# Two chunked recurrences: small TensorE products ordered by tile shape, and in-chunk products made once per 128 tokens

## The reference

```
A = where(causal, q_in @ k_in^T, 0)            # inside one chunk
o = A @ v + q_in @ S_prev                      # in-chunk part + part from the state
S = dec * S_prev + k_out^T @ v                 # the state that goes on
```

```
sa = S_t-1 a_t
S_t = S_t-1 * w_t + sa b_t^T + v_t k_t^T
y_t = S_t r_t
```

## Time and profile before

| | |
|---|---|
| median of 3 runs | 3005.89 us (3000.68 to 3006.42) |
| the profiled execution | 2999.36 us |
| its span, first to last instruction | 2997.6 us |
| mean granted TensorE clock | 0.93 |
| stage of the recurrences, first step 1 to the last step 8 | 917.28 to about 981.9 us |

### The profile page before, as it was taken

One profiled execution on the slowest core, in us unless ns is written; L12 is line 12 of the kernel. 1 busy time (PEld: TensorE's weight loads), 2 busy tenths in 40 slices (PEclk: granted clock), 3 DMA queues, 4 the chain that ended last, 5 costly groups with the idle time before them and its releaser, 6 DMA issues. The chain is left out here.

```text
span 2997.6 us, 61808 instructions
## 1 busy us (share of the span) xinstructions
PE 2594.2 (87%) x22240; PEld 2419.3 (81%) x22240; DVE 1988.2 (66%) x4119; ACT 1347.4 (45%) x2439; POOL 643.0 (21%) x506
## 2 busy tenths in 40 slices
PE   5798677798399589999999999866899999999998
PEld 2598556468397588999988899865899999988997
DVE  5501632341652469599999966546596899999765
ACT  5632334234320265655544455523555555444554
POOL 0144124227200379100000000162593000000000
PEclk9899779799696799999999999987999999999999
DMA  9522012115100234544434355421344544443452
GB/s 302 179 91 79 1 39 75 59 57 156 42 1 1 72 132 163 180 157 155 161 141 146 140 180 184 136 89 36 128 168 168 169 154 154 145 148 141 171 193 98
DMA packets 153851, 374.20 MB, mean 125 GB/s; under 512 B 8656, under 2 KB 102880, under 8 KB 137088
## 3 DMA queue, kind: packets, MB, share of 16 engines
q1 hardware_dynamic: 150784, 367.59, 36.1%
q10 hardware_dynamic: 2944, 4.98, 0.5%
HBM read 371.49 MB, written 1.05 MB: 124 GB/s over the span
## 5 line engine op out<-in xcount | busy, mean ns | idle before, releaser
L2413 ACT ACTIVATE w_hi<-ring 128x512 fp32r<-128x512 f32 x1024 | 643.6, 631 | 779.7 <-PE bank L2468 417.4
L2419 DVE TENSOR_TENSOR w_lo<-ring,w_hi 128x512 fp32r<-128x512 f32 x864 | 572.2, 690 | 207.7 <-ACT w_hi L2413 194.7
L360 POOL TENSOR_TENSOR w_lo<-ring,w_hi 128x512 fp32r<-128x512 f32 (+2 forms) x264 | 328.5, 1258 | 1340.4 <-ACT w_hi L351 1328.8
L2450 PE MATMUL bank<-x_hi,w_hi 128*128 128x256 f32 x2048 | 591.8, 289 | 20.4 <-POOL w_lo L2419 19.7
L2468 PE MATMUL bank<-hidden_hi,w_hi 128*128 128x256 f32 x2048 | 579.4, 283 | 34.3 <-issue 21.4
L2450 PE MATMUL bank<-x_lo,w_hi 128*128 128x256 f32 x2048 | 579.2, 283 | 0.0
L2450 PE MATMUL bank<-x_hi,w_lo 128*128 128x256 f32 x2048 | 578.9, 283 | 0.0
L2468 PE MATMUL bank<-hidden_hi,w_lo 128*128 128x256 f32 x2048 | 569.7, 278 | 0.0
L2468 PE MATMUL bank<-hidden_lo,w_hi 128*128 128x256 f32 x2048 | 569.2, 278 | 0.0
L2468 PEld LDWEIGHTS bank<-hidden_hi,w_hi 128*128 128x128 f32 x2048 | 383.8, 187 | 45.9 <-issue 29.9
L2450 PEld LDWEIGHTS bank<-x_hi,w_hi 128*128 128x128 f32 x2048 | 392.8, 192 | 24.2 <-ACT w_hi L2413 18.0
(11 more groups left out here) (519 smaller groups left out, 4460.8 us busy)
## 6 DMA issues: line engine op xcount, KB each, us to landing
ring<-in_peer_uT SPq DMA_DIRECT2D x128, 1024.0 KB, 4.9
ring<-in_peer_v SPq DMA_DIRECT2D x128, 1024.0 KB, 4.8
ring<-in_even_w_in SPq DMA_DIRECT2D x26, 1024.0 KB, 5.2
ring<-in_ada_w SPq DMA_DIRECT2D x24, 1024.0 KB, 8.8
ring<-in_odd_w_in SPq DMA_DIRECT2D x12, 1024.0 KB, 5.3
ring<-in_even_w_out SPq DMA_DIRECT2D x8, 1024.0 KB, 5.1
ring<-in_odd_w_out SPq DMA_DIRECT2D x8, 1024.0 KB, 5.1
ring<-in_peer_w_q SPq DMA_DIRECT2D x8, 1024.0 KB, 5.4
```

What stands on the lines that cost most here:

```text
L360: eng.tensor_tensor(k.lo[g % PARTS][:, 0:n], src, k.hi[g % PARTS][:, 0:n].bitcast(F32), ALU.subtract).then_inc(k.lo_ready, 1)
L2413: act.activation(k.hi[q][:, :], k.ring[slot][:, q * PART:q * PART + PART], ACT.Copy).then_inc(k.hi_ready, 1)
L2419: eng.tensor_tensor(k.lo[q][:, :], k.ring[slot][:, q * PART:q * PART + PART], k.hi[q][:, :].bitcast(F32), ALU.subtract).then_inc(k.lo_read ...
L2450: mm = pe.matmul(k.bank[s][:, j * T:j * T + T], a[q][:, w], b[:, cc, :], start=(cc == 0 and n == 0), stop=(cc == KC - 1 and n == 2))
```

## The change

In step 2 the four `AT` products come first, and only in the even chunks (c = 0 and 2), where they are made for all 128 rows of the half at once (tile shape 128*128); the `gqi` products of every chunk are then added onto the chunk's own 64 rows. In step 6 the eight `MrkT` products are treated in the same way, ahead of the `rt` products. The mark that starts a new sum in a bank (`start`) moves to the first product of each bank in the even chunk. No wait, no other engine's work and no DMA is changed.

```diff
--- before.py
+++ after.py
@@ -1879,12 +1879,13 @@
 
                 if c:
                     pe.wait_ge(outs_out, 4 * c - 2)
+                if c % 2 == 0:
+                    for h in range(4):
+                        pe.matmul(k.bank[(4, 7)[h % 2]][:, (h // 2) * P:(h // 2) * P + P], b["AT"][:, unit(m, h, 4), :],
+                                  b["gv"][:, m, h * P:h * P + P], start=(h < 2), stop=False, skip_group_check=True)
                 for h in range(4):
-                    o = k.bank[(4, 7)[h % 2]][r, (h // 2) * P:(h // 2) * P + P]
-                    pe.matmul(o, b["gqi"][rows(h), h // 2, t], b["S"][rows(h), h // 2, :],
-                              start=True, stop=False)
-                    mm = pe.matmul(o, b["AT"][:, unit(m, h, 4), r], b["gv"][:, m, h * P:h * P + P],
-                                   start=False, stop=True)
+                    mm = pe.matmul(k.bank[(4, 7)[h % 2]][r, (h // 2) * P:(h // 2) * P + P], b["gqi"][rows(h), h // 2, t],
+                                   b["S"][rows(h), h // 2, :], start=False, stop=(h >= 2), skip_group_check=True)
                 mm.then_inc(outs, 1)
                 for h in range(4):
                     mm = pe.matmul(k.bank[5][rows(h), (h // 2) * P:(h // 2) * P + P], b["gkoT"][r, m, h * 64:h * 64 + 64], b["gv"][r, m, h * P:h * P + P],
@@ -1905,10 +1906,12 @@
 
                 if c:
                     pe.wait_ge(outs_out, 4 * c)
+                if c % 2 == 0:
+                    for h in range(8):
+                        pe.matmul(half(2, 6, h), b["MrkT"][:, unit(m, h, 8), :], b["v"][:, m, h * 64:h * 64 + 64],
+                                  start=(h < 2), stop=False, skip_group_check=True)
                 for h in range(8):
-                    o = half(2, 6, h)[r, :]
-                    pe.matmul(o, b["rt"][rows(h), h // 2, t], b["Z"][rows(h), h // 2, :], start=(h < 2), stop=False, skip_group_check=True)
-                    pe.matmul(o, b["MrkT"][:, unit(m, h, 8), r], b["v"][:, m, h * 64:h * 64 + 64], start=False, stop=False,
+                    pe.matmul(half(2, 6, h)[r, :], b["rt"][rows(h), h // 2, t], b["Z"][rows(h), h // 2, :], start=False, stop=False,
                               skip_group_check=True)
                 pe.wait_ge(s2_out, c + 1)
                 for h in range(8):
```

## The result

The changed kernel took 2969.39 us (median of 4 runs, 2961.87 to 2969.7) where the kernel before took 3006.15 (4 runs, 3000.68 to 3007.4). The ratio is 0.9875, with a 95% interval of 0.9855 to 0.9895: 37 us faster, with a saving of 33.65 forecast. The profiled execution has a span of 2960.1 us, 37.5 less than before.

What follows compares the result with a forecast made beforehand. The prediction took TensorE's 64.7 us stage as the bound; its pieces, with the clock rising in chunk 0, gave 31 us, saving 33.65 from 3005.89, so 2972 us, range 2961 to 2989.

Steps and rivals of the forecast that it cites:

- The stage bounds and nothing runs ahead behind it: TensorE is busy throughout the 64.7 us stage, so a microsecond saved there is one saved in the whole.
- The pause belongs to the change of shape: Changing tile shape with every product costs about 0.2 us in step 6, up to 0.4 in step 2, low clock.
- The pieces: Prices of a chunk's products and waits: even 14.6, odd 8.9 us at the low clock; 8.35 and 5.55 high.
- The wait for U: Step 7 waits for ScalarE's U in odd chunks: 0.2 us at the low clock, 0.4 to 0.5 high.
- a wait of step 1 for `Z`: After step 8, VectorE's update of `Z` would hold the next work about 0.2 us a chunk at the high clock.
- what the doubling saves is shape changes, not passes: A full-height `AT` pass costs no less than two half-height products at step 5's rate, 0.85 us each.
- The clock: TensorE's clock rises within the first chunk, some 6 us in, and stays high; chance 0.62, or by chunk 0's end.
- low throughout: Rival: clock stays low through the whole stage, 47.0 us, saving 17.7, time 2988 us; chance 0.12.
- up and down: Rival: clock alternates, half the stage's work at either level, 37.4 us, saving 27.3, time 2979 us; chance 0.20.
- The sum: Stage pieces with the clock rising in chunk 0: 30.3 us, 34.0 if at its end; 31 taken, saving 33.65.
- slower: Rival: the expert layers behind the stage lose more to a low clock than the stage saves; chance 0.03.
- without effect: Rival: pause belongs to row-group changes or adding onto a sum just written; stage 60 us, time 3001; chance 0.03.

Runs made afterwards that it cites:

- other place: Kernel before, shapes still alternating, but no product added onto the place the product before it had just written; 3006.01 us in one run, stage 64.63 us.
- `MrkT` in step 8: Changed kernel with the `MrkT` products taken out of step 6 and made at half height in turn with `MrbT`; 2971.03 us in one run, stage 29.88 us.
- step 6 only: Kernel before with only step 6 (`rt` and `MrkT`) as in the changed kernel; 2982.64 us in one run, stage 42.65 us.
- double only: Kernel before with `AT` and `MrkT` made at full height in even chunks but products not grouped by shape; 2982.46 us, ratio 0.9936, stage 46.45 us.
- in pairs: Kernel before with the products of steps 2 and 6 ordered two by two, half the shape changes; 2980.94 us in one run, stage 41.77 us.
- once more: Kernel before, unchanged, profiled in another execution; 3005.35 us in one run, stage 64.66 us.
- diagonal tiles: Changed kernel with each full-height product made as two 64*64 products, `gqi` behind step 5, ScalarE copying U first; 2959.25 us, ratio 0.9839, stage 25.34 us.
- group only: Changed kernel with grouping but without doubled height, `AT` and `MrkT` at half height in every chunk; 2966.01 us, ratio 0.989, stage 31.49 us.
- step 2 only: Kernel before with only step 2 (`gqi` and `AT`) as in the changed kernel; 2976.6 us in one run, stage 43.26 us.
- full height together: Changed kernel with `AT` directly before `MrkT` behind step 5, then `gqi`, and ScalarE copying U first; 2966.94 us, ratio 0.9889, stage 30.09 us.

## Why the prediction was right

**The stage bounds and nothing runs ahead behind it.** Right: 35.3 of the 37.5 us between the two profiles are in the stage, and the idle time behind it is as long as before.

**The pause belongs to the change of shape.** Right, shown from both sides: alternation without a common place kept all of it (other place), a common place without alternation had none (`MrkT` in step 8). Each change that went gave back 0.40 us in step 2, as derived. In step 6 it gave back 0.28 and not 0.2; the prediction's own price of grouped `rt`, 0.10 us a product, has the rest in it, so its sum held.

**The pieces.** At the high clock the even chunk took 8.19 us (8.35 predicted) and the odd ones 5.32 and 5.43 (5.55); chunk 0 took 10.44 (10.8). At the low clock no whole kernel tested the prices, but chunk 0 of step 6 only (16.79 against 16.5) and of double only (20.11 against 20) did. `MrkT` merged took 1.92 with its change (1.8 for the passes alone), `AT` 1.08 (0.9). The wait for U came in the odd chunks alone, 0.35 us each (0.4 to 0.5). It was worked out with ScalarE's start 1.19 us behind step 5 at the high clock. Step 5 starts at 959.42 in the earlier trace rows; the line of ScalarE, from the timeline of the kernel before, is

```profile
960.61 0.59 ACT L1965 ACTIVATE small<-bank 64x512 f32<-64x512 f32 x1 [1.33 <-PE bank L1902]
```

and in the changed kernel the distance is 1.18 (929.63 to 930.81).

**A term that did not come.** The prediction added 0.2 us to each chunk at the high clock for a wait of step 1 for `Z`. The list of waits has none: in chunk 1 VectorE's last instruction on `Z` starts at 932.64 and lasts 0.43, so `Z` is ready at 933.07, and step 1 starts at 933.14, right behind step 8. Over the three chunks at the high clock this is 0.6 of the 0.9 us between the 30.3 us that the pieces add up to and the 29.38 measured.

**Wrong, without effect on the sum:** "what the doubling saves is shape changes, not passes". That about holds for `MrkT` and not for `AT`, with 128 columns streamed: its half-height pass (0.106 us at the high clock) is nearly as long as a full one (0.12), where a half-height pass of `MrkT`, with 64 columns, takes 0.06. `AT` was priced at step 5's rate, a pass with 64 columns. By the kernel with grouping alone the doubling is worth 1.0 us a half, the fewer passes of `AT` included and the wait for U already taken off. The sum for the change doesn't use that price, so the forecast didn't suffer.

**The clock.** Right that it would rise within chunk 0, some 6 us in (it was 4.9), and stay high. The reason given was stronger than what it rested on, two falls in one profile. No fall was seen where step 6 was grouped or in pairs, but with step 2 changed alone two alternating steps 6 passed at the high level without one. So that an alternating step 6 makes the clock fall is not shown; that without it no fall came is, and in this the forecast was partly lucky.

An estimate puts the clock's share beside that of the order. Had the clock been high throughout in both kernels, a chunk of before would cost 8 x 0.36 for step 2, 16 x 0.26 for step 6 and 4.0 for the rest, 11.0 us, four of them 44; four of grouping alone would cost 29 (7.27 each), and of the changed kernel 27. So of the 35 us some 17 would be saved at the high level too, 15 by the order and 2 by the doubled height, and the other half is the clock. The rivals "low throughout" and "up and down" are out for this kernel, in two executions of it. With step 2 changed alone, the second of them is what happened.

**The sum** said 31 us of stage; 29.38 came. The rivals "slower" and "without effect" have nothing left: the expert layers did not get longer (from their first instruction of line 2542 to the last they are 2.4 us shorter).

## What to carry to other kernels

On TensorE, count the changes of tile shape in a stream of small float32 matmuls before counting the matmuls: here each change that went gave back 0.3 to 0.4 us at the low clock, as much as three or four 64-column passes, and ordering the same products by shape took the stage from 64.65 to 31.5 us with no product saved. About half of that is the clock, which was low for most of the stage before and rose 5 us after its start with the products grouped. Neither can be seen in the busy time (TensorE showed 100% busy throughout): the pauses are read from the distance between starts, the clock from the granted share. Where a product's operand has zeros beside diagonal blocks, two 64*64 products in the two halves of the array were cheaper here than one of full height (0.93 us against 1.92 for `MrkT`); they were issued in turn and onto different banks.

## What the runs showed that was not expected

- The clock's course was the same in three executions (before, once more, and other place: chunks of 18.60, 18.39, 13.87 to 13.88 and 13.77 to 13.79 us), although the stage began at 916.56, 917.28 and 917.27 us; in two of the changed kernel chunk 0 differed by 0.02 us. In all of them the fall before the stage also came 8.7 us ahead of it, so it can't be told whether the course follows the work or the time since that fall; in diagonal tiles it came 10.4 us ahead, and the rise came 1.6 us earlier in the stage than in the changed kernel. Every fall seen inside the stage began in an alternating step 6 or 0.75 us behind it, but not every alternating step 6 brought one. None came where step 6 was grouped or in pairs, though step 2 alternated, singly or in pairs, at the high clock there. What exactly makes the clock rise or fall is left open. From the start of the stage the rise took 3.3 us in diagonal tiles, 4.9 to 5.0 in the changed kernel, group only, step 2 only and `MrkT` in step 8, 8.2 in full height together, 18.6 in step 6 only and in pairs, 22.0 in double only, and 39.0 in the kernel before and in other place.
- A half-height float32 pass (128*64) with 128 columns streamed took nearly as long as a full one (0.106 and 0.12 us at the high clock, `AT`); with 64 columns it took half as long (0.06 and 0.12, `MrkT`).
- Step 1's way of using the two halves of the array in turn carried over to diagonal tiles: 32 passes of 64*64 in 0.93 us, 0.03 each.
